# Decoder layer on one core: the last gate's prompt tiles in pairs, by seven half-size products

## The reference, cut to what matters

```python
    h = rms_norm(x, lp["norm_ffn"])
    x = x + (jax.nn.silu(h @ lp["w_gate"]) * (h @ lp["w_up"])) @ lp["w_down"]
    x = x + jax.nn.sigmoid(rms_norm(x, lp["norm_ple"]) @ lp["w_ple_gate"]) * (pe @ lp["w_ple_proj"])
    return x, c_kv, k_pe, new_conv
```

## Time and profile before

| what | value |
|---|---|
| median of 3 runs | 1662.71 us (1662.66 to 1665.81) |
| profiled execution, its own time | 1667.17 us |
| its span | 1665.4 us, 1.77 us less than its time |
| PE busy | 1638.9 us, 98% of the span |
| DVE busy | 1233.1 us, 74% |
| ACT, POOL busy | 672.1 us (40%), 518.4 us (31%) |
| granted PE clock, mean | 0.995 |

### The profile page before, as it was taken

The page is one execution under the profiler, slowest core; times in us unless marked ns, Lnnn a source line. Parts: engine busy times, 40 slices in busy tenths (PEclk is TensorE's granted clock), DMA queues, the critical chain, the costliest instruction groups (busy, mean ns, idle before and its releaser), DMA issues.

```text
span 1665.4 us, 28927 instructions
## 1 busy us (share of the span) xinstructions
PE 1638.9 (98%) x10629; PEld 1476.4 (89%) x10629; DVE 1233.1 (74%) x1879; ACT 672.1 (40%) x1270; POOL 518.4 (31%) x341
## 2 busy tenths in 40 slices
...
DMA packets 155919, 172.37 MB, mean 104 GB/s; under 512 B 35156, under 2 KB 107377, under 8 KB 155679
## 3 DMA queue, kind: packets, MB, share of 16 engines
...
...
## 4 chain that ended last, share of the span: by engine, by line
PE 83%; DVE 11%; issue 2%; POOL 1%; ACT 1%; SPq 1%; DMA 0%; DVEq 0%; ACTq 0%; POOLq 0%
PE ps L2729 22%; PE ps L2731 22%; PE ps L2730 22%; DVE arena L2282 2%; DVE arena L1856 2%; PE ps L3197 1%; PE ps L3019 1%; PE ps L2992 1%; PE ps L637 1%; PE ps L2735 1%; PE ps L2736 1%; PE ps L2972 1%; POOL stats L1006 1%; PE ps L2978 1%; DVE pT_lo L2173 1%
## 5 line engine op out<-in xcount | busy, mean ns | idle before, releaser
L1161 POOL TENSOR_TENSOR arena<-arena,mhalf 128x32 f32<-128x32 f32 (+1 forms) x40 | 180.6, 4521 | 114.1 <-DVE arena L2287 114.1
L2729 PE MATMUL ps<-cw_hi,pT_hi 128*128 128x288 f32 x512 | 164.0, 320 | 1.2 <-DVE pT_lo L2173 0.8
L1856 DVE SCALAR_TENSOR_TENSOR arena<-arena,tapw 128x1024 f32<-128x1024 f32 x120 | 159.6, 1330 | 1.8
L2503 DVE TENSOR_TENSOR dn_lo<-dn_raw,dn_hi 128x1024 fp32r<-128x1024 f32 x83 | 116.4, 1412 | 59.9 <-ACT dn_hi L1759 58.8
L2729 PE MATMUL ps<-T_hi,S_hi 128*128 128x272 f32 x528 | 152.3, 288 | 3.3 <-DVE U L2410 1.7
L2731 PE MATMUL ps<-T_hi,S_lo 128*128 128x272 f32 x528 | 152.0, 288 | 0.0
L2730 PE MATMUL ps<-F_B_r,S_hi 128*128 128x272 f32 x528 | 151.8, 287 | 0.0
L2730 PE MATMUL ps<-cw_lo,pT_hi 128*128 128x288 f32 x512 | 150.8, 294 | 0.0
L2731 PE MATMUL ps<-cw_hi,pT_lo 128*128 128x288 f32 x512 | 150.7, 294 | 0.0
L1759 ACT ACTIVATE dn_hi<-dn_raw 128x1024 fp32r<-128x1024 f32 x83 | 87.6, 1060 | 133.1 <-DMA dn_raw<-in_w_down 64.4
L2729 PE MATMUL ps<-dn_hi 128*128 128x512 f32 x308 | 120.0, 390 | 0.2 <-DVE U L2410 0.2
...
## 6 DMA issues: line engine op xcount, KB each, us to landing
dn_raw<-act_mid SPq DMA_DIRECT2D x77, 256.0 KB, 2.9
arena<-in_cache_ckv SPq DMA_DIRECT2D x128, 128.0 KB, 2.1
dn_raw<-in_w_down SPq DMA_DIRECT2D x45, 256.0 KB, 3.5
...
act_mid<-arena SPq DMA_DIRECT2D x11, 1024.0 KB, 8.3
wt_mid<-arena SPq DMA_DIRECT2D x11, 1024.0 KB, 4.2
```

The lines of the kernel that those rows point to most:

```text
L1161: nc.gpsimd.tensor_tensor(rstd_k[:, g0:g1, :], ms_k[:, g0:g1, :], mhalf[:, 0:(g1 - g0) * NH].rearrange("p (g h) -> p g h", h=NH), ALU.pow) ...
L1856: ins = nc.vector.scalar_tensor_tensor(y_of(c), glu[:, c, k:k + SEQ], tapw[:, c, k:k + 1], y_of(c), ALU.mult, ALU.add)
L2503: nc.vector.tensor_tensor(dn_lo_r[s], dn_raw[s], dn_hi[s][0], ALU.subtract).then_inc(s_("a_split"), 1)
L2729: mm(out, left[0], right[0], start=start, stop=False)
```

## The change

The order of tiles becomes 2, sample, 3, 4, 5, 0, 1, 6, 7. The first three (2, sample and 3; `PLAIN`) are done as before. The other six go in three pairs ("twins") of a tile u and a tile v. Of a pair, u gives the blocks A11 and A12 (its 512 lower and upper rows of the normed, transposed activations), v gives A21 and A22; `w_ple_gate` is split into B11, B12, B21, B22 of 512 x 512. Seven products, P1 = A11 B11, P6 = S2 T2, P2 = A12 B21, P5 = S1 T1, P7 = S3 T3, P3 = S4 B22 and P4 = A22 T4, each of 4 steps x 3 split products = 12 matmuls of 128x512, give C11, C12 (the gate of u) and C21, C22 (that of v).

- **Weights.** DVE forms T1 = B12-B11, T2 = B22-T1, T3 = B22-B12 and T4 = B21-T2 in the down projection, for four pieces k of 128 rows, two instructions at a time (`t_sums_of`, at the steps of `T_SUM_AT`), into two staging blocks in turn. SP stores each piece to a scratch tensor `t_mid` (1 MB each, `T_STORE_AT`) and loads T2, T1 and T3 (1 MB each) behind the down projection's last loads, T4 behind the third gate. ACT and DVE split them (`high_t`, `low_t`, 128x2048 each). POOL still makes the low halves of the plain weights, but starts only when the last weight sum is formed, since it overwrites the raw weights. The loads of the second half of `w_pg` move ahead of those of `w_pp`.
- **Activations.** The gain of u is applied by ACT in eight 128x128 pieces (`gain_u`), that of v by DVE (`gain_v`); DVE forms S1 = A21+A22, S2 = S1-A11, S3 = A11-A21, S4 = A12-S2; ACT makes the seven high halves, DVE the seven low halves.
- **Results.** ACT copies P1 out of PSUM; DVE makes U2 = P1+P6, C11 = P1+P2, V5 = U2+P5, C22 = V5+P7, U3 = U2+P7, C12 = V5+P3, C21 = U3+P4, each 128x512. ACT takes the sigmoid of each quarter, DVE multiplies and adds as before, by halves.
- **Order on TensorE.** P1, P6, P2, P5, transposes of the next u, P7, transposes of the next v, projection of u, P3, P4, projection of v. The transposes of the first u stand in the middle of the third gate.

The diff, cut to its core (in `T_SUM_AT` a step of the down projection is mapped to a piece and to its first or second half):

```diff
-PLE_TILES = [2, 3, 4, 5, 0, 1, 6, TILES, 7]
+PLE_TILES = [2, TILES, 3, 4, 5, 0, 1, 6, 7]
+PLAIN = 3
+TWINS = [(PLAIN + 2 * q, PLAIN + 2 * q + 1) for q in range((NT - PLAIN) // 2)]
+G_PRODUCTS = ["P1", "P6", "P2", "P5", "P7", "P3", "P4"]
...
+G_BANK = {"P1": 3, "P6": 4, "P2": 3, "P5": 7, "P7": 4, "P3": 7, "P4": 4}
+G_RESULTS = ["U2", "C11", "V5", "C22", "U3", "C12", "C21"]
...
+G_ENDS = [["u0", "u1", "v1", "v0"]] * 2 + [["u0", "u1", "v0", "v1"]]
+T_SUMS = ["T1", "T2", "T3", "T4"]
+T_LOADS = ["T2", "T1", "T3", "T4"]
+T_SEM = {"T2": "gate_loaded0", "T1": "gate_loaded1", "T3": "side_loaded", "T4": "gate_loaded0"}
...
+        T_SUM_AT = {dn_first("P7") + 9: (0, 0), dn_first("P7") + 10: (0, 1), dn_first("P5") + 4: (1, 0), dn_first("P5") + 5: (1, 1),
+                    dn_first("P5") + 6: (2, 0), dn_first("P5") + 7: (2, 1), dn_first("P5") + 10: (3, 0), dn_first("P4"): (3, 1)}
+        T_STORE_AT = [dn_first("P5") + 6, dn_first("P4") + 1, dn_first("P4") + 3, dn_first("P4") + 7]
...
+                for k in range(KC // 2):
+                    if i == T_STORE_AT[k]:
+                        sp.wait_ge(s_("sum_ready"), T_SUMMED(k, "T4"))
+                        if k % 2 == 0:
+                            sp.dma_start(t_mid[k].rearrange("b p n -> p b n"), t_sums).then_inc(s_("mid_stored"), 16)
+                        else:
+                            for n in range(len(T_SUMS)):
+                                sp.dma_start(t_mid[k, n], t_parts[1][n]).then_inc(s_("act_stored0"), 16)
+
+            def load_t(name):
+                sp.dma_start(T_full[name][0], t_mid[:, T_SUMS.index(name)].rearrange("k p n -> p k n")).then_inc(s_(T_SEM[name]), 16)
+            for k in (2, 3):
+                sp.wait_ge(s_(T_STORE[k % 2]), T_STORED(k))
+            for i, name in enumerate(("T2", "T1", "T3")):
+                sp.wait_ge(s_("prod_done"), dn_step_done(len(DN_STEPS) - DN_RING + i))
+                load_t(name)
...
+                    if j == PLAIN - 1:
+                        sp.wait_ge(s_("pg_done"), PLAIN)
+                        load_t("T4")
...
             def low_pp(k):
+            pool.wait_ge(s_("sum_ready"), T_SUMMED(KC // 2 - 1, "T4"))
...
+            def high_t(name):
+                act.wait_ge(s_(T_SEM[name]), T_LOADED(name))
+                if name == "T2":
+                    act.wait_ge(s_("prod_done"), dn_step_done(len(DN_STEPS) - 1))
+                nc.scalar.activation(T_hi[name][1], T_full[name][0], ACT.Copy).then_inc(s_("w_high"), 1)
+
+            def gain_u(q):
+                j = TWINS[q][0]
+                act.wait_ge(s_("c_xT"), NT + j + 1)
+                if q >= 1:
+                    act.wait_ge(s_("h4_split"), G_LOWS(q - 1, "A22"))
+                for b in range(2):
+                    for k in range(KH):
+                        g = COLS["norm_ple"][0] + KH * b + k
+                        last = nc.scalar.activation(G_full[0][("A11", "A12")[b]][0][:, k, :], ps[:, b, k * P:(k + 1) * P], ACT.Copy, scale=gcol[:, g:g + 1])
+                last.then_inc(s_("c_hT"), 1)
+                act.wait_ge(s_("c_hT"), G_GAINED(j))
+                high_a4(q, "A11")
+                high_a4(q, "A12")
+
...
+            for q, (u, v) in enumerate(TWINS):
+                more = q + 1 < len(TWINS)
+                act.wait_ge(s_("prod_done"), G_DONE(q, "P1"))
+                act.wait_ge(s_("y_ready"), G_ENDED(q - 1, "u0") if q else PLAIN)
+                nc.scalar.activation(sg[:, 0:HALF], ps[:, G_BANK["P1"], :], ACT.Copy).then_inc(s_("p1_copied"), 1)
+                if more:
+                    if q >= 1:
+                        act.wait_ge(s_("y_ready"), G_ENDED(q - 1, "v0"))
+                    x_square(u + 2, NT + v + 1, sg_v)
+                    act.wait_ge(s_("c_sumsq"), NT + u + 3)
+                    x_square(v + 2, 0, sg_v)
+                gate_of(q, "C11")
+                if q == 0:
+                    high_t("T4")
+                if more:
+                    gain_u(q + 1)
+                gate_of(q, "C22")
...
+            def t_sums_of(k, half):
+
+                out = dict(zip(T_SUMS, t_parts[k % 2]))
+                if half == 0:
+                    if k == 0:
+                        dve.wait_ge(s_("w_pg_loaded0"), 64)
+                        dve.wait_ge(s_("w_pg_loaded1"), 64)
+                    if k >= 2:
+                        dve.wait_ge(s_(T_STORE[k % 2]), T_STORED(k - 2))
+                    nc.vector.tensor_tensor(out["T1"], w_pg[0][:, k, HALF:DM], w_pg[0][:, k, 0:HALF], ALU.subtract).then_inc(s_("sum_ready"), 1)
+                    dve.wait_ge(s_("sum_ready"), T_SUMMED(k, "T1"))
+                    nc.vector.tensor_tensor(out["T2"], w_pg[1][:, k, HALF:DM], out["T1"], ALU.subtract).then_inc(s_("sum_ready"), 1)
+                else:
+                    nc.vector.tensor_tensor(out["T3"], w_pg[1][:, k, HALF:DM], w_pg[0][:, k, HALF:DM], ALU.subtract).then_inc(s_("sum_ready"), 1)
+                    dve.wait_ge(s_("sum_ready"), T_SUMMED(k, "T2"))
+                    nc.vector.tensor_tensor(out["T4"], w_pg[1][:, k, 0:HALF], out["T2"], ALU.subtract).then_inc(s_("sum_ready"), 1)
...
+            def low_t(name):
+                dve.wait_ge(s_("w_high"), T_HIGH(name))
+                nc.vector.tensor_tensor(T_full[name][1], T_full[name][0], T_hi[name][0], ALU.subtract).then_inc(s_("b_dve"), 1)
...
+            def result_4(q, name):
+                p, base, out = {"U2": ("P6", sg[:, 0:HALF], g_u2), "C11": ("P2", sg[:, 0:HALF], sg[:, 0:HALF]), "V5": ("P5", g_u2, g_v5),
+                                "C22": ("P7", g_v5, sg_v[:, HALF:DM]), "U3": ("P7", g_u2, g_u2), "C12": ("P3", g_v5, sg[:, HALF:DM]),
+                                "C21": ("P4", g_u2, sg_v[:, 0:HALF])}[name]
+                if name == "U2":
+                    dve.wait_ge(s_("p1_copied"), PAIRS + q + 1)
+                elif name in ("V5", "C22", "C21"):
+                    dve.wait_ge(s_("c_done"), G_MADE(q, {"V5": "U2", "C22": "V5", "C21": "U3"}[name]))
+                dve.wait_ge(s_("prod_done"), G_DONE(q, p))
+                nc.vector.tensor_tensor(out, base, ps[:, G_BANK[p], :], ALU.add).then_inc(s_("c_done"), 1)
...
+                    u, v = TWINS[0]
+                    nt_dve_mean(dve, "c", NT + v + 1, P, G_COL(v))
+                    dve.wait_ge(s_("c_xT"), NT + u + 1)
+                    x_scale(v)
+                    low_t("T1")
+                    low_t("T3")
+                    low_a4(0, "A11")
+                    gain_v(0)
+                    for name in G_SUMS:
+                        sum_a4(0, name)
+                    low_a4(0, "S2")
...
+            for name in G_LOW[2:]:
+                low_a4(0, name)
+            for q, (u, v) in enumerate(TWINS):
+                more = q + 1 < len(TWINS)
+                result_4(q, "U2")
+                if more:
+                    nt_dve_mean(dve, "c", NT + u + 3, P, G_COL(u))
+                    x_scale(u + 2)
+                    nt_dve_mean(dve, "c", NT + v + 3, P, G_COL(v))
+                result_4(q, "C11")
+                result_4(q, "V5")
+                if more:
+                    dve.wait_ge(s_("c_xT"), NT + u + 3)
+                    x_scale(v + 2)
+                if q == 0:
+                    low_t("T4")
+                result_4(q, "C22")
+                result_4(q, "U3")
+                if more:
+                    gain_v(q + 1)
+                    for name in ("S1", "S2", "S3"):
+                        sum_a4(q + 1, name)
+                    low_a4(q + 1, "A11")
+                end_4(q, "u0")
...
+                    if j == PLAIN - 1 and k == KH:
+                        nt_pe(pe, "c", NT + j + 2, P, xn4, 0)
...
+            def gate_product(q, name):
+                left, right = G_LEFT[name], G_RIGHT[name]
+                pe.wait_ge(s_("h4_split"), G_LOWS(q, left))
+                if q == 0 and right[0] == "T":
+                    pe.wait_ge(s_("b_dve"), len(B_DVE) + 1 + T_LOADS.index(right))
+                a = (G_hi[left][1], g_lo_a11 if left == "A11" else G_full[q % 2][left][1])
+                for k in range(KH):
+                    last = split_mm(ps[:, G_BANK[name], :], (a[0][:, k, :], a[1][:, k, :]), (G_B[right][0][:, k, :], G_B[right][1][:, k, :]),
+                                    start=k == 0, stop=k == KH - 1)
+                last.then_inc(s_("prod_done"), 1)
+
+            for j in range(PLAIN):
+                gate_tile(j)
+                if j + 1 < PLAIN:
+                    nt_pe(pe, "c", NT + j + 2, rows_of(PLE_TILES[j + 1]), xn4, 0)
+                else:
+                    pe.wait_ge(s_("c_hT"), G_GAINED(TWINS[0][0]))
+                    nt_pe(pe, "c", NT + TWINS[0][1] + 1, P, xn4, 0)
+                proj_tile(j)
+            for q, (u, v) in enumerate(TWINS):
+                more = q + 1 < len(TWINS)
+                if q == 0:
+                    pe.wait_ge(s_("sg_ready"), PLAIN)
+                else:
```

(67 more changed lines are left out.)

175 lines of the change are left out of this document (138 added, 37 removed).

## The result

| what | before | after |
|---|---|---|
| median | 1665.59 us (1662.66 to 1667.22, 6 runs) | 1670.41 us (1669.13 to 1671.42, 6 runs) |
| span of the profiled execution | 1665.4 us | 1669.3 us |
| first matmul of the first gate | 1531.96 us | 1542.72 us |
| last matmul | 1661.03 us | 1664.88 us |

The changed kernel is slower by 4.8 us: ratio 1.0032, 95% interval 1.0021 to 1.0043. The forecast was faster by 6.9 us. (Executions of one kernel differ by some 3 us with their mean granted clock, in the kernel before 0.999 in those near 1662.5 us and 0.995 to 0.998 in the longer ones, and two of the three behind the forecast's 1662.71 were short; with more runs it has 1665.5 to 1665.7.)

A forecast was written before the change was run, and what follows sets the result against it. The prediction took the number of TensorE's instructions to bound the end: -8.2 for fewer matmuls, +0.5 and +0.8 for waits, down projection at nothing, -6.9 from 1662.71, so 1655.8 us; own range 1654.5 to 1657.5, 8 in 10: 1653.8 to 1659.4.

The forecast's parts named there:

- the forecast's 1662.71: Median of the kernel before, in us, from which the forecast subtracted 6.9.
- The last stage: Gates and projections of the tiles: fewer matmuls and two added TensorE waits, together -6.9 us.
- -8.2 for 36 matmuls: Gates of the three pairs: 36 matmuls fewer at 0.227 us each, 8.2 us gained.
- a wait of 0.3 for VectorE's scale (`xn_late`) is there where 0.5 was forecast: Transposes of the first u, inside the third gate: TensorE waits 0.5 us for VectorE's chain.
- 0.8 for ACT's gains: First pair: TensorE cannot transpose the next v before ACT's gains and waits 0.8 us.
- The down projection at nothing: Down projection: 16 weight sums, 11.1 us on VectorE, costed at nothing through free steps and VectorE's lead.
- in P4 it meets the same slow steps as before: Down projection: with GpSimd's low halves moved to about 1429 to 1461, VectorE is quicker in P5, as slow in P4.
- 13.44 / 7 = 1.92: Down projection: mean time in us of a VectorE low half beside GpSimd's low halves, read from the old trace.
- GpSimd blocks VectorE: Rival, down projection: low halves take 4.3 a step against 2.72, 12 us late, 8.0 covered: 1659.8 us; chance 0.03.
- The 8.0 us of lead: Down projection: VectorE's low half for P5's ninth step is done 8.0 us before it is wanted, covering the sums.
- Sums, stores and loads: Down projection: weight sums, 4 MB of stores and the moved loads make TensorE wait for nothing; slower by stores: chance 0.07.

The follow-up runs named there:

- short sums: Changed kernel with VectorE's 16 weight sums cut to 8 columns each, GpSimd's low halves whole: 1668.89 us, 1.0020 of the kernel before.
- the other order: Changed kernel with the addition of P4's first tile ahead of two low halves in VectorE's list, GpSimd unchanged: 1663.80 us, 0.9987 of the kernel before.
- the filling: Changed kernel with 33 matmuls, product thrown away, in TensorE's list ahead of the wait for P4's first tile: 1668.09 us.
- VectorE's low halves: Changed kernel with GpSimd's ten low halves moved to VectorE, six in P4, four in P3: 1658.97 us, 0.9959 of the kernel before.
- short low halves: Changed kernel with GpSimd's ten low halves of the weights cut to 8 columns each: 1658.49 us, 0.9958 of the kernel before.
- 4.3 in the old kernel: Kernel before with only GpSimd's low halves made to wait for the low half of P4's fifth step: 1672.47 us, 1.0037 of the kernel before.

## Why the prediction was wrong

*The last stage* was right: -8.2 for 36 matmuls, back to -6.9 with the waits; measured -6.91, and 122.1 to 122.2 us again in the runs with short sums, with the other order, with the filling and with VectorE's low halves. The terms inside it were not all right: a wait of 0.3 for VectorE's scale (`xn_late`) is there where 0.5 was forecast, none of 0.8 for ACT's gains. Most of the rest is pace: counted over the records of both traces, 207 of TensorE's starts in this stage come 0.228 to 0.26 us behind the one before, 132 in the old kernel, which adds 0.6 us that no term had. That fewer matmuls give the gain was right; that the sum was hit to the tenth was luck.

*The down projection at nothing* failed, at one sentence: "in P4 it meets the same slow steps as before". Three things were wrong in it, and the first two could have been read from the trace of before.

First, the price. 13.44 / 7 = 1.92 is a mean over two kinds: GpSimd ended at 1433.30 + 12.44 = 1445.74, and these seven run to 1451.35, so some ran beside it and some alone. The stretch ahead of it has the blocked kind alone, 9.63 / 3 = 3.21 us, and the end of the seven the free kind, 3.48 / 3 = 1.16 (VectorE, kernel before):

```profile
1417.12 9.63 DVE L2503 TENSOR_TENSOR dn_lo<-dn_raw,dn_hi 128x1024 fp32r<-128x1024 f32 x3 [0.40 <-ACT dn_hi L1759]
...
1446.74 3.48 DVE L2503 TENSOR_TENSOR dn_lo<-dn_raw,dn_hi 128x1024 fp32r<-128x1024 f32 x3
```

The argument that set the rival "GpSimd blocks VectorE" at 0.03 rested on this mean and on there being no wait in P4. The Trainium skill (SBUF — State Buffer, Who interferes with whom) had the rule that the prediction set aside, exclusion for a whole instruction; with 3.19 beside GpSimd and 1.22 alone the runs agree with it.

Second, the cover. The 8.0 us of lead belong to the low halves. The addition of a finished tile has next to none: it becomes possible when P4's first tile is done, is wanted by P3's first matmul under 2 us later, and stands in VectorE's list behind the low halves for P3's first three steps. In the kernel before it was VectorE that waited there:

```profile
1453.92 0.69 DVE L2638 TENSOR_TENSOR arena<-arena,ps 128x512 f32<-128x512 f32 x1 [0.50 <-PE ps L2731]
```

Before, GpSimd was done 10 us ahead of that border (1445.74 against 1455.76), and VectorE used them to catch up, with halves of 1.22; that is why there was no wait in P4, not because VectorE was hardly slowed. The size could have been estimated from rows of before: eleven halves in P4 at 3.2 are 35 us for a product of 11 x 2.72 = 29.9, some 5 us late. The rows of the changed kernel give it as measured: the first three of the eleven took less (up to 2.24), but the other eight, 25.5 us, and the addition, 0.7, had 18.5 us: 7.7 late. The rival had 12 - 8.0 = 4.0: its 4.3 for a low half was too much, and the lead that it took off was not there for the addition.

Third, the clock: 2.16 us after the idle stretch stood in no term, though every us of TensorE waiting was priced at one.

*Sums, stores and loads* at nothing: right as waits of their own (with short low halves TensorE waits for none of them). But some 2 us of VectorE's lead went with the stores or the moved loads, and once GpSimd's stretch stood at the border that became idle time of TensorE, part of the 7.7 against 4.3 in the old kernel. The question asked of GpSimd's late low halves was who needs their result (the first gate, 70 us later); the one that mattered was who is slow beside them, and what stands behind that.
